# Decoding the expert numbers of a route: both sides in one 512-column pass, six VectorE instructions for nine

## The reference, cut to what matters

```python
s = jnp.einsum('thcd,hcnd->thcn', q, subkeys)          # two sides c, 128 keys each
s1, i1 = lax.top_k(s[:, :, 0], 16)
s2, i2 = lax.top_k(s[:, :, 1], 16)
cand = (s1[..., :, None] + s2[..., None, :]).reshape(T, 8, 256)
sc, ci = lax.top_k(cand, 16)
e = take_along_axis(i1, ci // 16, -1) * 128 + take_along_axis(i2, ci % 16, -1)
g = jax.nn.softmax(sc, axis=-1)
z = einsum('thkd,td->thk', u[e], h)                    # 16 rows of u per token and head
out = einsum('thk,thkd->td', gelu(z) * g, v[e])        # 16 rows of v
```

## Time and profile before

| | us |
|---|---|
| median of 3 runs | 1265.69 |
| lowest and highest | 1260.09, 1267.82 |
| the profiled execution | 1264.27 |
| its span in the trace | 1262.5 |
| DVE busy in it (x1848) | 919.4 |

### The profile page before, as it was taken

One profiled execution on the slowest core, in us unless ns is written; L12 is line 12 of the kernel. 1 busy time (PEld: TensorE's weight loads), 2 busy tenths in 40 slices (PEclk: granted clock), 3 DMA queues, 4 the chain that ended last, 5 costly groups with the idle time before them and its releaser, 6 DMA issues.

```text
span 1262.5 us, 14930 instructions
## 1 busy us (share of the span) xinstructions
PE 1142.1 (90%) x5180; PEld 797.5 (63%) x5180; DVE 919.4 (73%) x1848; ACT 511.4 (41%) x992; POOL 328.7 (26%) x316
## 2 busy tenths in 40 slices
PE   5999999999899998988778878887789999999998
PEld 4989999998655454443333433332335897788887
DVE  5997987786869667777677766677756696888544
ACT  3657443554423222221222222221524477677442
POOL 4000000000446444544454454454433000000000
PEclk9999999999999999999998999899989999999999
DMA  8874577588999999999999999999997622555550
GB/s 352 335 283 185 179 293 279 208 318 325 363 424 393 426 424 426 426 426 425 426 426 426 425 426 426 426 426 425 427 423 309 232 101 73 195 195 176 197 200 34
DMA packets 58703, 406.70 MB, mean 322 GB/s; under 512 B 7012, under 2 KB 7220, under 8 KB 10500
## 3 DMA queue, kind: packets, MB, share of 16 engines
q0 software_dynamic: 39184, 273.55, 51.9%
q1 hardware_dynamic: 19444, 132.19, 28.3%
HBM read 404.66 MB, written 1.06 MB: 321 GB/s over the span
## 4 chain that ended last, share of the span: by engine, by line
PE 58%; DMA 25%; DVE 9%; issue 4%; ACT 3%; POOL 1%; SPq 0%; DVEq 0%; POOLq 0%; ACTq 0%
PE bank L858 15%; DMA row_place<-in_peer_uv,ei 8%; DMA ring<-in_peer_uv,ei 6%; PE bank L496 5%; PE bank L500 5%; PE bank L497 5%; DMA gbuf<-in_peer_uv,ei 5%; PE bank L1017 5%; DMA wq_place<-in_peer_uv,ei 4%; PE bank L781 3%; PE bank L1020 2%; PE bank L1047 2%; PE bank L1048 2%; PE bank L1049 2%; PE bank L521 2%
## 5 line engine op out<-in xcount | busy, mean ns | idle before, releaser
L858 PE MATMUL bank<-gbuf,dg 128*128 128x512 f32 x504 | 247.2, 632 | 60.2 <-ACT dg L1356 58.1
L1550 DVE TENSOR_TENSOR half<-ring,half 128x1024 fp32r<-128x1024 f32 x175 | 212.7, 1222 | 85.1 <-ACT half L1073 83.1
L1073 ACT ACTIVATE half<-ring 128x1024 fp32r<-128x1024 f32 x173 | 181.7, 1055 | 126.4 <-PE bank L1049 47.0
L858 PEld LDWEIGHTS bank<-gbuf,dg 128*128 128x128 f32 x504 | 98.1, 200 | 193.9 <-issue 112.6
L2042 DVE CUSTOM_DVE_ANT_0 gbuf<-gbuf,h2t 128x1024 f32<-128x1024 f32 x126 | 154.4, 1225 | 72.2 <-DMA gbuf<-in_peer_uv,ei 68.1
L2398 POOL DMA_INDIRECT gbuf<-in_peer_uv,ei x123 | 140.4, 1141 | 172.7 <-PE bank L858 107.7
L1348 ACT ACTIVATE za<-za 128x4 f32<-128x4 f32 x62 | 12.7, 205 | 401.9 <-DVE za L2042 401.9
L858 PE MATMUL bank<-ring,dg 128*128 128x512 f32 x260 | 131.1, 633 | 17.3 <-ACT dg L1356 13.0
L496 PE MATMUL bank<-hh,half 128*128 128x256 f32 x448 | 113.1, 290 | 0.6 <-DVE hl L1708 0.3
L2042 DVE CUSTOM_DVE_ANT_0 ring<-ring,h2t 128x1024 f32<-128x1024 f32 x65 | 79.7, 1225 | 46.5 <-DMA ring<-in_peer_uv,ei 43.9
L497 PE MATMUL bank<-hl,half 128*128 128x256 f32 x448 | 110.5, 284 | 0.0
(11 more groups left out here) (446 smaller groups left out, 1999.7 us busy)
## 6 DMA issues: line engine op xcount, KB each, us to landing
ring<-in_weights SPq DMA_DIRECT2D x116, 1024.0 KB, 5.3
gbuf<-in_weights SPq DMA_DIRECT2D x4, 1024.0 KB, 9.8
gbuf<-in_peer_uv,ei POOLq DMA_INDIRECT x129, 14.8
bcs<-in_b_ada POOLq DMA_DIRECT2D x3, 512.0 KB, 12.3
ring<-in_peer_uv,ei POOLq DMA_INDIRECT x65
xs<-in_x SPq DMA_DIRECT2D x2, 512.0 KB, 4.0
ya<-in_weights SPq DMA_DIRECT2D x1, 1024.0 KB, 18.0
qkT<-in_weights SPq DMA_DIRECT2D x1, 1024.0 KB, 20.0
```

What stands on the lines that cost most here:

```text
L858: r = e.matmul(acc[a][j][:, :], dg[:, i % 4, :], expert_rows(i)[:, 1024 + 512 * j:1536 + 512 * j], start=h == 0 and k == 0, stop=h == 7 an ...
L1073: e.activation(h, v, AF.Copy).then_inc(*o.inc(*highs_of(n)))
L1550: e.tensor_tensor(l, v, h.bitcast(f32), ALU.subtract).then_inc(*o.inc(s_lov, split(n)))
```

## The change

For routes 1 to 15 the decoding handles both sides together. Two small instructions split the places into 32 columns of `pku` (side 0, then side 1), one comparison, one multiplication and one sum run over 32x16 = 512 columns, and the last instruction makes `ei` as before. These are six instructions in place of nine. The comparison now takes the columns 512 to 1023 of `pk`, where `cm2` lay, which is done with by then. The number of steps stays the same, but their contents differ. The second 8 experts of route 0 keep the old code, now called `decode_rest`. `pku` grows from 64 to 80 columns.

```diff
-    pku = st("pku", [128, 64], u32)
+    pku = st("pku", [128, 80], u32)
...
-            def decode(k0, k1):
+            def decode():
+
+                both, at = p[:, 512:1024], iu[:, 48:80]
+                for c in range(2):
+                    e.tensor_scalar(at[:, 16 * c:16 * c + 16], iu[:, 32:48], (4, 15)[c], None,
+                                    (ALU.logical_shift_right, ALU.bitwise_and)[c]).then_inc(*o.inc())
+                t = o.now
+                yield
+                e.wait_ge(*t)
+                e.tensor_tensor(both.rearrange("p (k a) -> p k a", a=16), at.unsqueeze(2).to_broadcast([128, 32, 16]),
+                                iota16[:, :].unsqueeze(1).to_broadcast([128, 32, 16]), ALU.is_equal).then_inc(*o.inc())
+                t = o.now
+                yield
+                e.wait_ge(*t)
+                by_side = both.rearrange("p (c k a) -> p c k a", c=2, a=16)
+                found = iu[:, 0:32].rearrange("p (c a) -> p c a", c=2).unsqueeze(2).to_broadcast([128, 2, 16, 16])
+                e.tensor_tensor(by_side, by_side, found, ALU.mult).then_inc(*o.inc())
+                t = o.now
+                yield
+                e.wait_ge(*t)
+                e.tensor_reduce(e12[:, 0:32], both.rearrange("p (k a) -> p k a", a=16), AX.X, ALU.add).then_inc(*o.inc())
+                t = o.now
+                yield
+                e.wait_ge(*t)
+                e.scalar_tensor_tensor(out=ei[:, a, 16 * h:16 * h + 16], in0=e12[:, 0:16], scalar=128.0, in1=e12[:, 16:32],
+                                       op0=ALU.mult, op1=ALU.add).then_inc(*o.inc(s_ei, n + 1))
+
+            def decode_rest(k0, k1):
...
-            yield from decode(8 if n == 0 else 0, 16)
+            yield from decode() if n else decode_rest(8, 16)
```

## The result

The changed kernel takes 1270.88 us in the median (1269.38 to 1273.05, 6 runs), the kernel before 1264.97 (1260.09 to 1267.82, 6 runs). The ratio is 1.0048 with a 95% interval of 1.0032 to 1.0063: slower by 5.9 us, where 0.7 us of gain was forecast, and 1.8 us above the range. The profiled execution took 1269.38 us, 5.1 more than that of before.

A forecast was written before the change was run, and what follows sets the result against it. Transfers at 426 GB/s were taken to set the pace, except from 385 to 405 us. There 0.36 + 0.36 us gave 1264.27 - 0.7 = 1263.6 us; 1.42 us more made the median 1265.0, range 1257.7 to 1269.1.

The forecast's parts named there:

- All later routes, 13 of the 15, I cost at nothing: Later routes' decoding savings were taken as hidden behind transfers at 426 GB/s; uncovered, they would be 8.5 us.
- Rival (d): Wide instructions run below full rate, costing up to 1.3 us in route 2 and behind; median 1267.0 us, chance 0.06.
- The weight 0.36 us earlier: In routes 1 and 2 the stretch from first split to weight shrinks from 0.54 to 0.18 us.
- 0.29 us less in the two groups behind: DVE's steps behind the next two dots of route 2 shrink by 0.11 and 0.18 us.
- the forecast 0.7 us: PE restarts 0.72 us earlier in route 2, shrinking the transfer gap by that much; chance 0.60.
- Rival (b): No gain arrives, since route 2's start hangs on something taken for hidden; median 1265.7 us, chance 0.12.
- rival (c): The saving counts in full in all 15 routes, 9.75 us; median 1255.9 us, chance 0.04.
- the thin stretch: From 385 to 405 us transfers fall below 426 GB/s, short of orders; at most 2.4 us to win back.
- POOL's wait of 0.42 us for `ei` in route 2: POOL's wait for L2017 near 387 us was to shrink to the usual gap, with `ei` ready at 386.19.
- The wait of 2.28 us before 570.44: Route 6: POOL was said to wait for `ei`, depending on a landing, absorbed while transfers hold 426 GB/s.
- the rule that spoke against the forecast: Two-SBUF-input VectorE instructions share a read interface with GpSimd and block it; set aside because issues averaged 1.15 and 1.17 us.
- rival (e): Two wide two-input instructions hold POOL 1.4 us in the thin stretch, net +0.7 us; median 1266.4 us, chance 0.04.

The follow-up runs named there:

- the tripled comparison: Changed kernel with `pku` at 128 columns and the 512-column comparison done three times, each behind the one before: 1262.22 us against 1263.8, ratio 0.9994.
- the kernel of the new decoding alone: Changed kernel with `pku` back at 64 columns, split places in their own tile behind `gbuf`, no old tile moved: 1261.44 us against 1262.85, ratio 0.9994.
- `pku` at 128: Changed kernel with `pku` at 128 columns in place of 80, so `gbuf` starts at a multiple of 256 bytes: 1264.27 us against 1265.65, ratio 0.9989.
- the small tiles moved: Kernel before with `ei`, `za`, `dg` and `g3` moved by 64 bytes and `gbuf` by 256: 1263.45 us against 1262.85, ratio 1.0002.
- the new decoding with all places aligned: Changed decoding, split places in their own tile, every gather target at a multiple of 256 bytes, against the kernel before: 1260.54 us against 1263.8, ratio 0.9975.

## Why the prediction was wrong

**The step that failed** is "All later routes, 13 of the 15, I cost at nothing: their cover is the transfers at 426 GB/s". The cover held, as the tripled comparison shows. What didn't hold was the rate: I took 426 GB/s for a given, and the change lowered it to 421. The diff's first hunk, `pku` at 80 columns, had no term in the sum at all. It should have had one: it moves the target of 126 gathers by 64 bytes, in the resource that sets the pace. Its measured size is a ratio of 1.0055 alone (1.0038 to 1.0072), 5.9 us between the medians. The prediction named a changed rate as what would show it wrong, but no case of it had that cause, and so the range ended at 1269.1. It also held that a measurement of this kernel tells only about 1% from no change; the interval of the result is 0.3% wide, and a loss of 0.48% lies clear of it.

**The steps that held,** with the changed profile and the kernel of the new decoding alone:

- Wide instructions at 0.69 us: 0.687, 0.687, 0.681, full rate also over the four-dimensional view. Rival (d) has fallen.
- The weight 0.36 us earlier in each of routes 1 and 2: 0.39 (0.54 to 0.15) in route 1, and PE's idle time at the restart in route 2 0.39 shorter. As spacings both are there; that they moved the times of day is another matter, see below.
- 0.29 us less in the two groups behind: from PE's restart to the start of the last instruction it was 387.03 - 382.95 = 4.08 us and is 386.81 - 383.05 = 3.76, so 0.32 less.
- A gain of the size of the forecast 0.7 us, from the new decoding without the moved `gbuf`: 1.4 between the medians of the new decoding alone and before (0.9994, 0.9983 to 1.0005), 1.4 with `pku` at 128 (0.9989, 0.9979 to 0.9998). The forecast (0.7 us is 0.9994) lies in both intervals. Rival (b), nothing arrives, is not excluded by the first and is by the second; rival (c), 9.75 us, is excluded by both. That the gain came by way of the thin stretch is not shown.

**Two misreadings that cost nothing.** The first is POOL's wait of 0.42 us for `ei` in route 2. I expected it to shrink, and it reads 0.55. It isn't a wait for that `ei` at all. In POOL's loop transfer number i, counted from 0, waits for `s_ei` of route i // 16. Counted from the first (at 317.64 us), the transfer at 387.42 is number 28, of route 1, whose `ei` had been complete since 353.13. Number 32, the first of route 2, starts at 397.27, 10.07 us after its `ei` was complete. The kernel with three comparisons settles it, for there number 28 starts before the `ei` of route 2 is even begun:

```profile
397.27 1.63 POOL L2398 DMA_INDIRECT wq_place<-in_peer_uv,ei  x1 [0.30 <-PE bank L858]
```

```profile
387.55 0.95 POOL L2431 DMA_INDIRECT ring<-in_peer_uv,ei  x1 [0.78 <-PE bank L858]
388.33 0.17 DVE L2028 SCALAR_TENSOR_TENSOR ei<-pk 128x16 uint32<-128x16 f32 x1
```

(The first line is of the kernel before, the other two of the one with three comparisons.) In each of them number 28 starts 4.47 or 4.48 us after PE's restart, so it goes by the places that PE frees. The wait of 2.28 us before 570.44 is misread in the same way: that is number 108, of route 6, whose `ei` was complete at 530.19. In the kernel before, every route from 1 to 15 has its `ei` complete 2.2 to 22 us ahead of the transfer that needs it, and so no part of the prediction that asks whether `ei` keeps up had anything to decide.

The second is the rule that spoke against the forecast, and rival (e). The means of 1.15 and 1.17 us hid a hold that is there. In the kernel before, 118 of POOL's 259 issues start while VectorE is inside an instruction with two inputs from SBUF (a dot, or a TENSOR_TENSOR or SCALAR_TENSOR_TENSOR) that has over 0.13 us to go. Of these, 112 last until 0.81 us after that instruction's end, to within 0.02 us, up to 1.98 us in all; the other six last 0.93 or 0.94 us. The 141 issues that start beside anything else, or nothing, last 0.93 to 1.03 us. The issue at 387.42 lasts 1.73 us, to 389.15, and this dot ends at 388.34; in the changed kernel dot and issue end at 388.12 and 388.93:

```profile
387.12 1.22 DVE L2042 CUSTOM_DVE_ANT_0 ring<-ring,h2t 128x1024 f32<-128x1024 f32 x1
```

```profile
386.90 1.22 DVE L2069 CUSTOM_DVE_ANT_0 ring<-ring,h2t 128x1024 f32<-128x1024 f32 x1
```

So the rule that I set aside holds in this trace, and that the rows fit an issue which needs the write interface alone was wrong: instructions with two inputs hold it up, and TENSOR_REDUCE and MAX8, with one, do not. It changed nothing between the two kernels, because most holds come from the dots, which both have alike: over 0.937 us an issue, they add up to 61.3 us before and 62.7 after. From 434 to 940 us an issue takes 1.17 and 1.18 us, and in the thin stretch POOL is busy 13.83 us for 12 and 13.23 for 13.

**Why the times of day did not move.** The chain of the changed kernel in route 1, against the earlier trace rows, and the granted clock of the two stretches around its start:

```profile
347.68 8.83 PE bank L858 x16
...
366.83 3.47 PE bank L781 x16
...
372.01 0.60 ACT sct L1330
```

```profile
340.00:350.00 10.00, 7.22 (x16) 2.92 (x15) 9.72 (x32) 1.49 (x5) 4.40 (x4) 0.94 1.02 422
350.00:360.00 10.00, 10.00 (x30) 5.96 (x29) 8.23 (x16) 3.28 (x9) 4.82 (x4) 0.89 1.01 421
```

L858's first 16 matmuls took 8.83 us in place of 7.13, at a clock of 0.94 and 0.89, a mean between the two levels of 1.2 and 2.4 GHz, behind 2.78 us in which PE was idle. So PE's early start was lost in this execution: the copy of the scores came at 372.01, and at 371.52 before. It isn't the decoding's doing. The kernel before with only `gbuf` moved (8.58 us) and with the small tiles moved (8.83) show the same slow 16 matmuls with old decoding, the one with `pku` at 80 columns doesn't (7.13), and neither does the new decoding with all places aligned (7.13).

With like paired with like the decoding's part can be read. From L858's start in route 1 to PE's restart in route 2 it is 35.76 us with the old decoding and slow matmuls (small tiles moved), and 35.37 in the changed kernel; with quick ones it is 34.07 before and 33.66 with the new decoding and all places aligned. So 0.4 us less each time, where 0.36 was forecast:

```profile
347.16 8.83 PE bank L859 x16
382.92 1.98 PE L859 MATMUL bank<-gbuf,dg 128*128 128x512 f32 x4 [1.14 <-ACT dg L1357]
```

```profile
346.98 7.13 PE bank L862 x16
380.64 1.99 PE L862 MATMUL bank<-gbuf,dg 128*128 128x512 f32 x4 [0.74 <-ACT dg L1360]
```

But over all profiled executions the restart lies anywhere from 380.64 to 386.22 us, and the thin stretch is no fixed 2.4 us: from 385 to 410 us the kernel before with `pku` at 80 columns and the one with `gbuf` 32 bytes off moved 422 and 420 GB/s, so nothing was missing, and the one with the small tiles moved only 379, with the same old decoding in all three. Against this a shift of 0.72 us can't be read from one profile, and whether it ends in the measured time stays open.

**The cause of the slower packets** is shown as far as this: the remainder of the target's address to 256 bytes, in gathers of rows of 8192 bytes, at equal cost for 32, 64 and 128. A likely mechanism is stated by the Trainium skill (DMA: Bandwidth & Descriptors, section How a descriptor splits into AXI transactions): a descriptor that starts at a multiple of 256 bytes is split into pieces of 256, and one that starts elsewhere has its first piece begin at the boundary below it, with the bytes ahead of its start fetched for nothing. An estimate from that page of the Trainium skill is 33 pieces for 32 for an unaligned row of 8192 bytes, 3.1% more; counted in its units of 32 bytes it would be 257, 258 and 260 for 256 at 32, 64 and 128 bytes off, 0.4 to 1.6% more. The measured packets grew by 314.0 / 309.4 = 1.5% at 64 and 128 bytes and by 1.6% at 32. That all three cost the same speaks for a price by the piece, but the size fits neither count. It is stated there of reads, and here the written side moved, so the mechanism is argued and not shown. Why unaligned rows cost next to nothing when half of the rows are aligned stays open: that a floor of 309 ns, set elsewhere, hides the extra of rows mixed with aligned ones fits the table, but no run tests it.

## What to carry to other kernels

- Where transfers set the pace, a size in an allocation is a change to the bound. Compare the addresses of the transfers' targets before and after a change, and keep them at multiples of 256 bytes; here one number was worth 5.9 us, eight times the 0.7 us that six instructions for nine were forecast to bring.
- Read the rate at full share, not only the share. Both kernels show 1.01 in the same stretch, and the loss stands in 421 against 426 GB/s and in the packets' own times. When a rate moves that the edited instructions shouldn't touch, try the parts of the diff one by one, the harmless-looking first.
- An engine that waits for landings can take on work for nothing: some 22 us more of it disappeared here.
- Before a wait is read, count which transfer it belongs to and what the code makes that one wait for. The profile named the `ei` of a route that the transfer doesn't need, and more than once.
- Don't read contention from means. Sort the instructions by what ran beside them when they started; here 1.15 and 1.17 us stood for 0.94 and up to 1.98.

## What the runs showed of the hardware that was not expected

- Gathers of 8192-byte rows whose targets in SBUF may lie at addresses 32, 64 or 128 bytes off a multiple of 256: with none aligned 314.0 to 314.4 ns a packet and 420 to 421 GB/s; with all aligned 309.4 ns and 427 GB/s; with half of them 310.2 and 426. With `gbuf` aligned, the unaligned `ring` and `wq_place` of the kernel before cost 0.8 ns a packet.
- An indirect transfer's issue on POOL, 0.94 us by itself, lasts until 0.81 us after the end of a VectorE instruction with two SBUF inputs that was running when it started (112 of 118 cases before, 121 of 126 in the changed kernel). MAX8, FIND_INDEX8, MATCH_REPLACE8 and TENSOR_REDUCE beside it lengthened none of them past 1.03 us.
- Two small VectorE instructions that don't depend on each other (0.17 us each alone) take 0.24 us together, 346.82 to 347.06, and the next one starts 0.15 us after the first.
- 16 matmuls of 128x512 in f32 after 2.8 to 3.2 us of idle PE took 7.13 us in four of the 14 profiled executions and 8.52 to 8.83 in the others. From 340 to 350 and from 350 to 360 us the granted clock was 1.00 in the quick ones; in each slow one it was 0.83 to 0.96 in at least one of the two. What decides between them is open.
